# Low parts of weight pieces in the mixers: two GpSimd instructions of 512 columns in place of four of 256

## The chip, the cores and the metric

One core of a Trainium2 chip runs the kernel. Its engines are TensorE (PE; its weight loads are shown apart as PEld), VectorE (DVE), ScalarE (ACT), GpSimd (POOL) and SyncE (SP), which issues the loads. The metric is the device time of one execution in microseconds; the median of the runs shown stands for the kernel.

## The reference

The reference is a chain of two small transformer networks on one sequence of 256 tokens with a width of 1024, two layers each, all in float32:

```python
for l in range(2):                       # first network
    x = x + 0.5 * rmsnorm(swiglu(rmsnorm(x), w_gate, w_up, w_down))     # hidden width 2816
    x = x + rmsnorm(token_mixing(rmsnorm(x), w_in, ..., w_out))         # three kinds of attention
    x = x + 0.5 * rmsnorm(swiglu(rmsnorm(x), ...))
for l in range(2):                       # second network
    z = rmsnorm(x) @ w_in
    merged = sum(gate_i * (branch_i(z) @ w_branch[i]) for i in range(3))
    x = x + merged @ w_out
    x = x + square(relu(rmsnorm(x) @ w_up)) @ w_down                    # hidden width 4096
```

The token mixing of the first network has chunk band attention, differential attention and stick-breaking attention side by side. The three branches of the second network are a sparse attention (compressed, selected and window keys), a gated linear attention and an attention over 256 memory tokens. Nearly all of the work is in the products with the weights.

## The kernel before

All weights come as one stream of 616 pieces of 128 partitions x 1024 float32 columns, in the order in which they are used. SP loads a piece into one of 7 slots of `raw` (line 478). ScalarE rounds it to the format that TensorE multiplies fast and writes the result, the high part, into one of 5 slots of `hi` (line 1509). GpSimd subtracts the high part from the piece and writes what is left, the low part, into a slot of `lo` (lines 615, 624 and 634). Activations are split in the same way, and a product is made of three matmuls, high with high, high with low and low with high (`product`, lines 660 to 663); a piece takes 12 matmuls of 512 columns as a rule. TensorE waits for a piece by the semaphore `lo`; after its last matmul on it, it raises `used`, for which the slots of `raw` and `hi` wait.

Each engine runs a program of its own, written out in order; the semaphores tie them together. In a feed-forward stage the pieces follow one another with little else between them. In a mixer (a function `in_mixer` says which pieces these are, line 586) the steps of the attention are placed behind chosen pieces: TensorE makes scores, transposes and sums between the pieces, and VectorE and ScalarE do softmax and the like meanwhile. Where TensorE reaches such a step before its input is made, it waits, and the pieces behind it wait too.

Which part of a low part GpSimd makes in one instruction depends on the place: a whole piece of 1024 columns outside the mixers, halves for a few pieces at the beginning of stages (`by_halves`), and quarters of 256 columns in the mixers. In the first network's mixers (`c < L * PIECES1`) GpSimd also waits for its own quarter, by the semaphore `quarter`, before it issues the next one; in the second network's mixers quarters follow each other freely. At the start of each mixer piece it waits for the end of the piece before (line 630).

The steps of the second network's mixer that come up later: line 2562 subtracts the reference points of the decay of the gated linear attention (four instructions for each half of the levels), lines 2571 and 2572 multiply queries and keys by the decay, lines 2258 and 2262 (`normalise`) scale softmax rows by the inverse of their sums, line 2251 (`minima`) takes scores out of PSUM, line 935 is TensorE's transpose of the finished rows (`turn_blocks`), and line 2270 VectorE's copy of what it turned. Lines 2614 to 2623 are the activation of the compressed keys' hidden layer, which TensorE multiplies in line 1276. In the first network's mixer, line 2373 squares the output of the differential attention. Line 2849 belongs to the rotary angles, which are made in the last strips of a feed-forward stage.

Of the kernel before, what the change touches and what calls it, by code (L numbers as in the profile page):

```python
# [220 lines left out]
def f32(a):  # L221
    return a.bitcast(F32)
# [356 lines left out]
def half_width(c):  # L579

    at = (c - L * PIECES1) % PIECES2 if c >= L * PIECES1 else 0
    z3 = 4 * STRIPS2.index("z3")
    return WIDTH_Z3 if z3 <= at < z3 + 4 else PIECE // 2


def in_mixer(c):

    block, at = divmod(c, PIECES1) if c < L * PIECES1 else divmod(c - L * PIECES1, PIECES2)
    if c < L * PIECES1:
        return FFN_PIECES + 6 <= at < PIECES1 - FFN_PIECES - 4  # L590
    return 12 <= at < PIECES2 - 8 * MLP_STRIPS - KD - 4


def by_halves(c):

    if c < L * PIECES1:
        return c % PIECES1 in (FFN_PIECES + 3, PIECES1 - FFN_PIECES + 3) or c > PIECES1 and c % PIECES1 == 3
    at = (c - L * PIECES1) % PIECES2
    return at in (3, PIECES2 - 8 * MLP_STRIPS - 1, PIECES2 - 8 * MLP_STRIPS + 3)
# [7 lines left out]
def pool_program(M, V, sem):  # L607

    pool = M.nc.gpsimd
    for c in range(FIRST_HALVES):  # L610
        for i in range(2):
            w = slice(512 * i, 512 * i + 512)
            raw = M.raw[:, c, w] if c else V.first_weights[i]
            pool.wait_ge(sem["hi" if i else "half_hi"], c + 1)
            pool.tensor_tensor(M.lo[:, c, w], raw, f32(M.hi[:, c, w]), ALU.subtract).then_inc(
                sem["lo"] if i else sem["half_lo"], 1)
    quarters = 0
    for c in range(FIRST_HALVES, PIECES):
        slot, slot_hi = c % RING, c % RING_HI
        pool.wait_ge(sem["hi"], c + 1)  # L620
        if by_halves(c):
            for i in range(2):
                w = slice(512 * i, 512 * i + 512)
                pool.tensor_tensor(M.lo[:, slot, w], M.raw[:, slot, w], f32(M.hi[:, slot_hi, w]),
                                   ALU.subtract).then_inc(sem["lo"] if i else sem["half_lo"], 1)
            continue
        parts = 4 if in_mixer(c) else 1
        if parts == 4:

            pool.wait_ge(sem["lo"], c)  # L630
        for i in range(parts):
            whole = 2 * half_width(c)
            w = slice(i * whole // parts, (i + 1) * whole // parts)
            t = pool.tensor_tensor(M.lo[:, slot, w], M.raw[:, slot, w], f32(M.hi[:, slot_hi, w]), ALU.subtract)  # L634
            if i == parts - 1:
                t.then_inc(sem["lo"], 1)
            elif c < L * PIECES1:

                t.then_inc(sem["quarter"], 1)
                quarters += 1  # L640
                pool.wait_ge(sem["quarter"], quarters)
# [2275 lines left out]
def build(nc, T):  # L2917
    with ExitStack() as stack:
        M = memory(nc, T, stack)
        V = Views(M)  # L2920
        sem = {name: stack.enter_context(nc.semaphore("s_" + name)) for name in SEMAPHORES}
        landed = [stack.enter_context(nc.semaphore(f"s_landed{i}")) for i in range(RING)]
        sp_program(M, V, sem, landed)
        pool_program(M, V, sem)
        pe_program(M, V, sem)
        act_program(M, V, sem, landed)
        dve_program(M, V, sem)
# [151 lines left out]
```

## Time and profile before

| | us |
|---|---|
| median of 3 runs | 1880.04 |
| the runs | 1879.98 to 1880.36 |
| the profiled execution | 1880.13 |
| its span, first to last instruction | 1878.70 |

| engine | busy us | share of the span | instructions |
|---|---|---|---|
| PE matmuls | 1872.5 | 100% | 9604 |
| PE weight loads | 1549.8 | 82% | 9604 |
| VectorE | 1033.4 | 55% | 2654 |
| ScalarE | 1035.0 | 55% | 1765 |
| GpSimd | 1555.6 | 83% | 1102 |

The profile shows one execution. Times within it count from the start of the span. The shares are means over stages of different kinds; matmuls overlap, so a busy PE is not a measure of how fast it goes. The mean granted clock of TensorE is 1.000 in this execution. The mixers of the first network lie at about 201 to 282 us and 682 to 762 us, those of the second at about 994 to 1204 us and 1447 to 1658 us.

### The profile page before, as it was taken

The numbers are of one execution on the slowest core, as the hardware profiler recorded it, in microseconds if no ns is written. First come the engines' busy times: TensorE is split into PE (matmuls) and PEld (weight loads), VectorE is DVE, ScalarE is ACT, GpSimd is POOL, SyncE is SP. The second block draws the span as 40 slices with busy tenths as digits, with TensorE's granted clock in tenths as the row PEclk, the third lists the DMA queues.
The fourth block names the chain that finished last, engine by engine and source line by source line (L and its number), as shares of the span: only waits on it lengthen the run. The fifth ranks groups of instructions, "written<-read, shape, count | busy, mean of one in ns | idle before, by whom it ended". The sixth has DMA issues, their size and how long they took to land.

```text
span 1878.7 us, 27088 instructions
## 1 busy us (share of the span) xinstructions
PE 1872.5 (100%) x9604; PEld 1549.8 (82%) x9604; DVE 1033.4 (55%) x2654; ACT 1035.0 (55%) x1765; POOL 1555.6 (83%) x1102
## 2 busy tenths in 40 slices
PE   9999999999999999999999999999999999999999
PEld 8888887888888889788888877888888877788887
DVE  5338565434676756554344677446444477645542
ACT  7445666444744576654466454665456554566543
POOL 8988886988798878698879787779887968778986
DMA  7665444565565553367556343456657533345553
GB/s 285 243 231 182 166 135 157 192 198 192 204 236 196 190 169 135 132 220 261 196 187 255 124 146 117 154 184 220 235 191 260 169 126 133 124 165 194 192 197 138
DMA packets 98419, 348.94 MB, mean 186 GB/s; under 512 B 13260, under 2 KB 13932, under 8 KB 97772
## 3 DMA queue, kind: packets, MB, share of 16 engines
q1 hardware_dynamic: 97708, 346.06, 54.0%
q8 instruction: 77, 1.26, 0.3%
q10 hardware_dynamic: 576, 1.14, 0.2%
q14 instruction: 58, 0.48, 0.1%
HBM read 346.11 MB, written 1.05 MB: 185 GB/s over the span
## 4 chain that ended last, share of the span: by engine, by line
PE 99%; DVE 1%; ACT 0%; issue 0%; ACTq 0%
PE psum L661 28%; PE psum L663 28%; PE psum L662 28%; PE psum L689 1%; PE psum L691 1%; PE psum L692 1%; PE psum L945 1%; PE psum L759 1%; PE psum L935 1%; PE psum L958 1%; PE psum L1204 1%; PE psum L925 0%; PE psum L1361 0%; PE psum L1155 0%; PE psum L832 0%; PE psum L828 0%
## 5 line engine op out<-in xcount | busy, mean ns | idle before, releaser
L634 POOL TENSOR_TENSOR lo<-raw,hi 128x256 fp32r<-128x256 f32 (+2 forms) x1070 | 1520.4, 1443 | 298.3 <-ACT hi L1509 270.4
L1509 ACT ACTIVATE hi<-raw 128x1024 fp32r<-128x1024 f32 (+1 forms) x613 | 639.1, 1052 | 495.7 <-PE psum L663 461.6
L661 PE MATMUL psum<-hi,h_hi 128*128 128x512 f32 (+1 forms) x1504 | 592.6, 394 | 0.0
L663 PE MATMUL psum<-hi,h_lo 128*128 128x512 f32 (+1 forms) x1504 | 583.6, 388 | 0.0
L662 PE MATMUL psum<-lo,h_hi 128*128 128x512 f32 (+1 forms) x1504 | 583.0, 388 | 0.0
L2211 DVE STREAM_TRANSPOSE psum<-big 32x128 f32<-32x128 f32 (+1 forms) x960 | 344.0, 358 | 14.2
L661 PEld LDWEIGHTS psum<-hi,h_hi 128*128 128x128 f32 x1504 | 282.5, 188 | 59.0 <-issue 2.1
L663 PEld LDWEIGHTS psum<-hi,h_lo 128*128 128x128 f32 x1504 | 282.3, 188 | 58.9
L661 PE MATMUL psum<-hi,y_hi 128*128 128x512 f32 x832 | 328.1, 394 | 0.0
L662 PEld LDWEIGHTS psum<-lo,h_hi 128*128 128x128 f32 x1504 | 282.7, 188 | 54.8
L663 PE MATMUL psum<-hi,y_lo 128*128 128x512 f32 x832 | 324.3, 390 | 0.0
L662 PE MATMUL psum<-lo,y_hi 128*128 128x512 f32 x832 | 323.9, 389 | 0.0
L2220 DVE TENSOR_TENSOR y_lo<-psum,y_hi 128x512 fp32r<-128x512 f32 x76 | 51.0, 689 | 327.8 <-ACT y_hi L1635 327.4
L661 PEld LDWEIGHTS psum<-hi,y_hi 128*128 128x128 f32 x832 | 156.2, 188 | 34.5 <-issue 2.5
L663 PEld LDWEIGHTS psum<-hi,y_lo 128*128 128x128 f32 x832 | 156.2, 188 | 33.1
L662 PEld LDWEIGHTS psum<-lo,y_hi 128*128 128x128 f32 x832 | 156.3, 188 | 31.1
L2199 DVE SCALAR_TENSOR_TENSOR big<-psum,small,big 128x256 f32<-128x256 f32 (+1 forms) x120 | 61.0, 550 | 87.9 <-ACT big L1625 87.8
L1675 ACT ACTIVATE soft<-soft,small 128x128 f32<-128x128 f32 (+1 forms) x104 | 47.2, 455 | 78.3 <-DVE small L2251 57.5
L1625 ACT ACTIVATE big<-psum,small 128x256 f32<-128x256 f32 (+1 forms) x120 | 57.3, 529 | 53.9 <-PE psum L663 53.8
L2270 DVE COPY soft<-psum 128x384 f32<-128x384 f32 (+1 forms) x52 | 29.8, 573 | 49.3 <-PE psum L935 49.3
L689 PE MATMUL psum<-h_hi,hi 128*128 128x256 f32 x192 | 56.1, 292 | 0.0
L691 PE MATMUL psum<-h_lo,hi 128*128 128x256 f32 x192 | 54.3, 283 | 0.0
(355 smaller groups left out, 1599.4 us busy)
## 6 DMA issues: line engine op xcount, KB each, us to landing
raw<-in_stream SPq DMA_DIRECT2D x607, 512.0 KB, 3.4
big<-in_w SPq DMA_DIRECT2D x14, 512.0 KB, 7.1
big<-in_post SPq DMA_DIRECT2D x6, 512.0 KB, 4.7
special<-in_b_merge SPq DMA_DIRECT2D x2, 1536.0 KB, 7.4
raw<-in_stream SPq DMA_DIRECT2D x8, 296.0 KB, 5.6
memkv<-in_mem_turned SPq DMA_DIRECT2D x2, 1024.0 KB, 6.9
big<-in_band SPq DMA_DIRECT2D x2, 768.0 KB, 4.9
raw<-in_first SPq DMA_DIRECT2D x2, 512.0 KB, 4.1
```

Of the source, the lines that this page charges most:

```text
L634: t = pool.tensor_tensor(M.lo[:, slot, w], M.raw[:, slot, w], f32(M.hi[:, slot_hi, w]), ALU.subtract)
L661: pe.matmul(out, lhs_hi, rhs_hi, start=start, stop=False)
L662: pe.matmul(out, lhs_hi, rhs_lo, start=False, stop=False)
L663: return pe.matmul(out, lhs_lo, rhs_hi, start=False, stop=stop)
L689: pe.matmul(out, hi[:, slot_hi, w], h_hi[:, k, :], start=k == 0 and block % 2 == 0, stop=False, skip_group_check=True)
L691: pe.matmul(out, hi[:, slot_hi, w], h_lo[:, k, :], start=False, stop=False, skip_group_check=True)
L1509: act.activation(M.hi[:, slot_hi, used], M.raw[:, slot, used], ACT.Copy).then_inc(sem["hi"], 1)
L1625: t = act.activation(act_s[:, m, :], psum[:, bank + m, 0:width], ACT.Silu if gated else ACT.Relu, scale=V.scale[:, m:m + 1])
L1675: t = act.activation(prob[:, w], prob[:, w], ACT.Exp, scale=-1.0, bias=mn[:, i:i + 1], accum_out=total[:, i:i + 1])
L2199: t = dve.scalar_tensor_tensor(prod_s[:, m, :], psum[:, bank + m, col:col + width], V.scale[:, m:m + 1], act_s[:, m, :], ALU.mult, ALU.mult)
L2211: t = dve.transpose(dst[32 * b:32 * b + 32, :, :, 32 * a:32 * a + 32], src[32 * a:32 * a + 32, :, :, 32 * b:32 * b + 32])
L2220: dve.tensor_tensor(flat(y_lo[:, kt:kt + 2, :]), psum[:, bank + g, :], f32(flat(y_hi[:, kt:kt + 2, :])), ALU.subtract).then_inc(sem["ylo"], 1)
```

## The change

In the mixers, a low part is made in two instructions of half the piece each in place of four of a quarter each. The waits in the loop stay as they are written: in the first network one wait for the own first half is left of three for own quarters.

```diff
-        parts = 4 if in_mixer(c) else 1
-        if parts == 4:
+        parts = 2 if in_mixer(c) else 1
+        if parts == 2:
 
             pool.wait_ge(sem["lo"], c)
         for i in range(parts):
```

## Rows read from the trace of the kernel before

**Rows 1.** The page, part 1: busy time, share of the span, instructions of each engine.

```profile
PE 1872.5 (100%) x9604; PEld 1549.8 (82%) x9604; DVE 1033.4 (55%) x2654; ACT 1035.0 (55%) x1765; POOL 1555.6 (83%) x1102
```

**Rows 2.** Timeline (start us, us, engine, line, operation) of PE, then PEld, at 301.

```profile
300.68 0.39 PE L662 MATMUL psum<-lo,y_hi 128*128 128x512 f32 x1
...
302.26 0.39 PE L663 MATMUL psum<-hi,y_lo 128*128 128x512 f32 x1
...
301.13 0.19 PEld L662 LDWEIGHTS psum<-lo,y_hi 128*128 128x128 f32 x1
```

**Rows 3.** Waits over the span: engine, line <- releaser: us in all, times, longest.

```profile
POOL lo L634 <- ACT hi L1509: 270.4, 229, 7.6
...
PEld psum L1276 <- DVE extra L2623: 1.5, 2, 0.8
...
PEld psum L689 <- POOL lo L634: 0.7, 2, 0.3
```

**Rows 4.** GpSimd's groups by shape: xcount | busy us, mean ns | idle before them.

```profile
L634 POOL TENSOR_TENSOR lo<-raw,hi 128x256 fp32r<-128x256 f32 x624 | 464.1, 766 | 114.5 <-ACT hi L1509 87.2 <-POOL lo L634 0.4
L624 POOL TENSOR_TENSOR lo<-raw,hi 128x512 fp32r<-128x512 f32 x22 | 28.0, 1294 | 6.3 <-ACT hi L1509 6.3
```

**Rows 5.** Timeline of GpSimd at 1092.55 us, one quarter.

```profile
1092.55 0.74 POOL L634 TENSOR_TENSOR lo<-raw,hi 128x256 fp32r<-128x256 f32 x1 [3.88 <-ACT hi L1509]
```

**Rows 6.** Timeline of GpSimd and VectorE in a feed-forward stage, at 562.6 us.

```profile
562.61 2.40 POOL L634 TENSOR_TENSOR lo<-raw,hi 128x1024 fp32r<-128x1024 f32 x1 [0.32 <-ACT hi L1509]
...
562.63 2.44 DVE L2849 SCALAR_TENSOR_TENSOR extra<-extra 128x48 f32<-128x48 f32 x1
```

**Rows 7.** Summaries of two lines: xcount, shortest/median/longest ns, first to last start.

```profile
L2849 DVE SCALAR_TENSOR_TENSOR extra<-extra x3: 207/1917/2444, 560.4 to 562.6; 128x48 f32<-128x48 f32 x3
...
L2373 DVE TENSOR_TENSOR special<-special x2: 846/860/874, 236.0 to 716.8; 128x512 f32<-128x512 f32 x2
```

**Rows 8.** Timeline of the second network's first mixer, 1054.3 to 1057.3 us.

```profile
1054.35 2.84 POOL L634 TENSOR_TENSOR lo<-raw,hi 128x256 fp32r<-128x256 f32 x4 [1.02 <-ACT hi L1509]
...
1054.49 0.67 DVE L2621 TENSOR_SCALAR extra<-extra 128x128 f32<-128x128 f32 x1
...
1055.20 0.95 DVE L2622 RECIPROCAL extra<-extra 128x128 f32<-128x128 f32 x1
...
1056.19 0.42 DVE L2623 TENSOR_TENSOR extra<-extra 128x128 f32<-128x128 f32 x1
...
1056.66 0.41 PE L1276 MATMUL psum<-special,extra 128*32 128x64 f32 x4 [0.51 <-DVE extra L2623]
```

**Rows 9.** VectorE's groups, 1083 to 1107 us: xcount | busy, mean ns | idle before.

```profile
L2572 DVE TENSOR_TENSOR big<-big,kT 128x1024 f32<-128x1024 f32 x2 | 3.5, 1756 | 0.0
```

**Rows 10.** Summary of line 2562, 1083 to 1088 us, columns as in rows 7.

```profile
L2562 DVE TENSOR_TENSOR big<-extra x4: 942/950/960, 1083.8 to 1086.4; 128x256 f32<-128x256 f32 x4
```

**Rows 11.** Timelines of GpSimd, VectorE and PE, 1082 to 1110 us.

```profile
1082.13 6.54 POOL L634 TENSOR_TENSOR lo<-raw,hi 128x256 fp32r<-128x256 f32 x8 [5.18 <-ACT hi L1509]
...
1093.29 0.85 DVE L2262 TENSOR_SCALAR soft<-soft,small,extra 128x256 f32<-128x256 f32 x1
...
1094.77 0.33 PE L935 MATMUL psum<-consts,soft 128*128 128x128 f32 x1
...
1105.31 0.87 DVE L2262 TENSOR_SCALAR soft<-soft,small,extra 128x256 f32<-128x256 f32 x1
...
1108.68 0.27 PE L935 MATMUL psum<-consts,soft 128*128 128x128 f32 x1
...
1109.21 0.56 DVE L2270 COPY soft<-psum 128x384 f32<-128x384 f32 x1 [2.48 <-PE psum L935]
```

**Rows 12.** Timelines of GpSimd, VectorE and PE, 1145 to 1149 us.

```profile
1145.67 2.91 POOL L634 TENSOR_TENSOR lo<-raw,hi 128x256 fp32r<-128x256 f32 x4 [7.59 <-ACT hi L1509]
...
1147.16 0.83 DVE L2262 TENSOR_SCALAR soft<-soft,small,extra 128x256 f32<-128x256 f32 x1
...
1148.29 0.27 PE L935 MATMUL psum<-consts,soft 128*128 128x128 f32 x1
```

## The prediction

> **What bounds the kernel now.** I read the shares of the engines first [rows 1]. TensorE (PE) is busy for 100% of the span, but a busy share says little where matmuls overlap, so the second view is a timeline of PE in a stretch without waits [rows 2]: from 300.68 to 302.26 us seven matmuls of 512 columns start, one every 0.226 us, each shown 0.39 us long. I take that pitch as PE's floor; the clock stands at its upper level all along, since the mean granted clock of the profiled run is 1.0.
>
> The Trainium skill, page "Trainium Kernel Development and Optimization", section "Performance Expectations", calls matmul busy time a bad metric and LDWEIGHTS busy share a good one; by that rule the 82% of [rows 1] would leave up to 18% to win. The trace speaks against it here: in [rows 2] a weight load takes 0.19 us of a pitch of 0.226, which is 83% with nothing waiting, so 82% over the span is the floor too.
>
> Third come the waits [rows 3]. GpSimd (POOL) waits 270.4 us for ScalarE's high parts, so it is ahead of its supply. PE waits for GpSimd's low parts 0.7 us in all. The longest wait of PE's weight loads for another engine is that of line 1276 for VectorE (DVE): 1.5 us in two times. So PE sets the end, and a change to GpSimd moves the time only through instants at which PE waits for VectorE or GpSimd. There is next to nothing to win, and something to lose where a hand-over to PE is tight.
>
> **What is removed and added.** The trace has 624 quarter instructions of 766 ns and, from pieces that are done by halves already, 22 of 512 columns of 1294 ns [rows 4]. 156 pieces are meant: 624 x 0.766 = 478 us go and 312 x 1.294 = 404 us come, so GpSimd has 74 us less to do. I count this at nothing: it lies beside PE, GpSimd waits for ScalarE longer than that now, and PE's waits for it are 0.7 us, which is all that could be won. If that cover were gone, a piece would still come sooner than before (2 x 1.29 against 4 x 0.74 [rows 5] or more), so it can't cost. In the first network's mixers one wait of GpSimd for its own quarters stays per piece where three were; nothing but GpSimd's next instruction is queued behind it. No DMA is moved: GpSimd issues none, and SP's loads wait for PE's use of a piece, not for GpSimd.
>
> **What gets longer: the time in which GpSimd shuts VectorE out.** Rows of the feed-forward stretch show it alone [rows 6, 7]: line 2849, 128x48, takes 207 ns undisturbed and 2444 ns when it starts 0.02 us after a GpSimd instruction of 2.40 us; it ends at 565.07, 0.06 us after that one. So a VectorE instruction of that kind (two operands in SBUF, or a plain SBUF-to-SBUF one) waits until the GpSimd instruction under way is over. An undisturbed quarter is 0.74 us, a half 1.29 [rows 4]; a wait that begins near the start of one grows by 0.55 us.
>
> The Trainium skill, page "SBUF — State Buffer", section "SBUF: two separate sides", says the same as a rule, which speaks against this change: the pair of ports shared by GpSimd and VectorE is "an exclusive lock, not a bandwidth split", held for the whole instruction. With shared bandwidth the number of columns per instruction would not matter and the sum below would be 0.
>
> In the first network's mixers only line 2373 waits, twice in the run, 846 and 874 ns long [rows 7]; what follows it is not needed by PE soon. I count 0, and 0.1 us at most. The second network's mixers (994 to 1204 us, and the same again from 1447) have three places; I read them in the first.
>
> Place one, around 1054 [rows 8]. Line 2621 starts 0.14 us into a quarter and lasts 0.67, to 1055.16; line 2622 takes 0.95; line 2623 starts at 1056.19, waits for the third quarter, which ends at about 1056.46 (a piece takes 2.84, so quarters start 0.70 apart), and ends at 1056.61; PE's line 1276, idle for 0.51 us, starts 0.05 us later. With halves from the same start (ScalarE's high part sets it) the first ends at 1055.64, so 2621 ends 0.55 later; 2623 then starts at 1056.74, and the second half ends at 1056.89, so 2623 ends at about 1057.04. PE idles already, so all of it counts: **0.43 us**. Bounds: 0 (the second wait vanishes and GpSimd starts late) and 0.55.
>
> Place two, 1083 to 1107. VectorE is without a pause: the 11 groups of its instructions there show 0.0 or 0.1 us idle before them, as the row in [rows 9] does, so each delay is handed on. GpSimd starts two pieces at 1082.13 and works until 1088.67 [rows 11]; line 2562's four instructions run from 1083.8 to 1087.35 with one quarter between each two [rows 10]. Halves end at about 1083.4, 1084.8, 1086.4 and 1087.8 (0.17 more for each VectorE instruction let in: line 2562's starts lie (1086.4 - 1083.8) / 3 = 0.87 apart, against 0.70 of a quarter); 2562 gets in after the second, third and fourth, the last one follows freely, and they end at 1088.4: 1.1 late. Then GpSimd starts at 1092.55 [rows 5]; its second half ends at 1095.1, and line 2262's pair, which ended at 1094.14, ends at 1095.5: 1.36 late [rows 11]. PE's transposes of line 935 need it and start at 1094.77, 0.63 after it: PE loses 0.73. Between that and line 2262's end at 1106.18, five more VectorE instructions wait for GpSimd now (lines 2571, 2572, 2262, 2572, 2262): 5 x 0.55 = 2.75, together 4.1 late, 1110.3. PE needs that one at 1108.68, now 1109.41: another 0.88. Sum **1.6 us**. Bounds: 0.5 (only the first loss, with two of the later five waits grown) and 3.5 (every wait grows by 0.55, those of 2562 too). I take the walk, since its instants come from rows; the ends of pieces, where GpSimd waits for its own semaphore (line 630) and VectorE can slip in, cut it below the upper end. Little is late after that: VectorE now sits idle for 2.48 us before its next copy [rows 11], which waits for the same transposes.
>
> Place three, around 1147 [rows 12]: GpSimd starts at 1145.67, so the second half ends at 1148.2; line 2262's second instruction, which ended at 1147.99, ends at 1148.4, and PE's line 935 at 1148.29 is 0.1 late. Bounds 0 and 0.6. **0.1 us**.
>
> Sum per mixer 0.43 + 1.6 + 0.1 = 2.15, and for two mixers 4.3 us. The profiled execution took 1880.13 us (span 1878.70 and 1.43 around it), 0.09 over the median of the runs, 1880.04. **1880.1 + 4.3 = 1884.4 us.** By the bounds 1880.1 + 2 x 0.5 = 1881.1 to 1880.1 + 2 x 4.65 = 1889.4. No loss is counted for PE's pitch: nothing in the trace ties it to the length of GpSimd's instructions.
>
> **Rivals.** (1) The delays of place two are absorbed: only place one counts, 0.43 x 2, and the time is 1881.0. For it: the first need has 0.63 us and the last 2.5 us of room [rows 11]; a shift of the start by some tenths, or one more pause of GpSimd, is enough. Against it: VectorE has no idle time there. (2) Place two costs its upper end, the others as forecast: 2 x (0.43 + 3.5 + 0.1) = 8.1, 1888.2. For it: 2562's four and the later waits each meet a fresh instruction in the trace of before; against it: with halves there are fewer of them to meet.
> (3) The other side, not slower: GpSimd, done with a piece in 2 x 1.29 us and not in 2.84, sits idle when VectorE comes, and waits vanish. Place one decides: VectorE waits there until 1055.09 and 1056.46, 0.60 and 0.27 us, more than PE's idle 0.51, which would go, 1.0 us in two mixers; the time is 1879.1. It decides from the point at which GpSimd would be through before 1054.49, but there it had been idle for 1.02 us and starts with ScalarE's high part at 1054.35 [rows 8], whatever it did before. (4) The change doesn't do what it says, and GpSimd shuts VectorE out no longer than before: 1880.1. Against it: instructions of 512 and 1024 columns of this form are in the trace, and the longest one held VectorE for all its 2.40 us [rows 6].
>
> **Chances.** The forecast has 0.52, rival 1 0.20, rival 2 0.16, rivals 3 and 4 together 0.12. A measurement of this kernel can tell about 0.2% from no change, 3.8 us, so slower begins at 1883.8. Seven tenths of the forecast's own case (1882 to 1887) and all of rival 2 lie above: 0.36 + 0.16 = 0.52 slower. Faster needs more than PE waits for in all, 0.03. The rest, 0.45, is the same. The range of 8 in 10 runs from rival 1, a little under, to the upper bound: 1880.8 to 1889.4.
>
> **What would show it.** Right: GpSimd has 312 more instructions of 512 columns near 1.3 us, and no fewer idle times; line 2621 takes about 1.2 us and PE's idle before line 1276 grows from 0.51 to about 0.9; line 2562's four in the busy place take about 1.4 us each and line 935's weight loads show waits for line 2262 of 0.7 to 0.9 us in two places; PE's pitch stays 0.226. Wrong: line 2562 or 2262 as short as before, PE's waits for VectorE unchanged, or lost time in the first network's mixers, where I count none. A new wait of PE for low parts would speak against the first part of the sum.

## The result and the profile after

| | before | after |
|---|---|---|
| median, us | 1880.03 | 1886.90 |
| the runs, us | 1879.98 to 1880.36 (6) | 1886.64 to 1887.12 (6) |
| the profiled execution, us | 1880.13 | 1886.64 |

The ratio is 1.0037, with an interval of 1.0027 to 1.0046: slower by 6.87 us, 0.37%, where 4.3 us were forecast and the range went from 1880.8 to 1889.4 us.

GpSimd did what the change says. Its groups by shape in the profile after (count | busy us, mean ns | idle before them), beside [rows 4]:

```profile
L634 POOL TENSOR_TENSOR lo<-raw,hi 128x512 fp32r<-128x512 f32 x312 | 413.2, 1340 | 169.1 <-ACT hi L1509 152.1 <-POOL lo L634 0.4
```

312 halves stand for the 624 quarters, GpSimd works 464.1 - 413.2 = 51 us less on them, and idles more before them (169.1 us, where it was 114.5). PE got nothing from that. Its waits for another engine in the profile after (us in all, times, longest):

```profile
PE psum L935 <- DVE soft L2262: 4.7, 6, 1.5
PE psum L1276 <- DVE extra L2623: 1.9, 2, 0.9
...
PE psum L661 <- POOL lo L634: 0.2, 1, 0.2
```

Line 935 waited for line 2262 nowhere before; line 1276's wait rose from 1.0 us (PE's own idle time) to 1.9. The one wait for a low part lies at 28 us, ahead of all mixers; nothing speaks of low parts that come late in them. So the time went where VectorE hands something to PE. How much at which place is read from the instants of the same PE instructions in the two timelines; first before, in the first of the two mixers, just ahead of it and behind it, and behind the second:

```profile
971.72 0.55 PE L759 MATMUL psum<-consts,x 128*128 128x128 f32 x3
...
1222.10 0.27 PE L759 MATMUL psum<-consts,big 128*128 128x128 f32 x1
...
1676.50 0.60 PE L759 MATMUL psum<-consts,big 128*128 128x128 f32 x4
```

and after, with that wait at 28 us and the three places between (those of before are in [rows 8, 11, 12]):

```profile
28.12 0.47 PE L661 MATMUL psum<-hi,h_hi 128*128 128x512 f32 x1 [0.17 <-POOL lo L634]
...
971.32 0.66 PE L759 MATMUL psum<-consts,x 128*128 128x128 f32 x4
...
1056.66 0.41 PE L1276 MATMUL psum<-special,extra 128*32 128x64 f32 x4 [0.94 <-DVE extra L2623]
...
1096.38 0.33 PE L935 MATMUL psum<-consts,soft 128*128 128x128 f32 x1 [1.47 <-DVE soft L2262]
...
1111.09 0.33 PE L935 MATMUL psum<-consts,soft 128*128 128x128 f32 x1 [0.64 <-DVE soft L2262]
...
1151.16 0.33 PE L935 MATMUL psum<-consts,soft 128*128 128x128 f32 x1 [0.24 <-DVE soft L2262]
...
1225.04 0.27 PE L759 MATMUL psum<-consts,big 128*128 128x128 f32 x1
...
1683.01 0.38 PE L759 MATMUL psum<-consts,big 128*128 128x128 f32 x2
```

| PE instruction | before | after | shift, us | lost since the row above | forecast |
|---|---|---|---|---|---|
| line 759, ahead of the mixer | 971.72 | 971.32 | -0.40 | | |
| line 1276, place one | 1056.66 | 1056.66 | 0.00 | 0.40 | 0.43 |
| line 935, place two, first need | 1094.77 | 1096.38 | 1.61 | 1.61 | 0.73 |
| line 935, place two, last need | 1108.68 | 1111.09 | 2.41 | 0.80 | 0.88 |
| line 935, place three | 1148.29 | 1151.16 | 2.87 | 0.46 | 0.1 |
| line 759, behind the mixer | 1222.10 | 1225.04 | 2.94 | 0.07 | 0 |
| line 759, behind the second mixer | 1676.50 | 1683.01 | 6.51 | 3.57 | 2.15 |

The last shift, 6.51, is the whole difference of the two profiled executions, 1886.64 - 1880.13. The first, -0.40, is not the change's doing: the execution after is 0.51 us ahead at 28 us already (28.12 for 28.63), in the first feed-forward stage, where nothing was changed. Without it the losses add up to 6.91 us, close to the 6.87 between the medians. The places are those of the forecast; two of the four terms are too small.

### The profile page after: what moved, and what is told of

It reads as the page before. It is cut to its first block, busy times and chain, and to the rows that moved or that the text cites. A ratio compares the mean times of both kernels' runs of the same rounds, so it can differ in the third digit from the quotient of the medians.

```text
span 1885.2 us, 26776 instructions
## 1 busy us (share of the span) xinstructions
PE 1872.9 (99%) x9604; PEld 1548.2 (82%) x9604; DVE 1051.7 (56%) x2654; ACT 1034.9 (55%) x1765; POOL 1504.9 (80%) x790
## 4 chain that ended last, share of the span: by engine, by line
PE 93%; DVE 4%; issue 1%; ACT 1%; DMA 1%; POOL 0%; SPq 0%; DVEq 0%; ACTq 0%
PE psum L661 27%; PE psum L663 27%; PE psum L662 27%; PE psum L689 1%; PE psum L691 1%; PE psum L692 1%; PE psum L759 1%; PE psum L945 1%; PE psum L935 1%; PE psum L1204 1%; PE psum L958 1%; DVE soft L2262 0%; DVE big L2572 0%; DVE big L2562 0%; PE psum L925 0%
## 5 line engine op out<-in xcount | busy, mean ns | idle before, releaser
L634 POOL TENSOR_TENSOR lo<-raw,hi 128x1024 fp32r<-128x1024 f32 (+2 forms) x758 | 1469.7, 1958 | 356.0 <-ACT hi L1509 338.5
L692 PE MATMUL psum<-h_hi,lo 128*128 128x256 f32 x192 | 54.3, 283 | 0.0
```

The costliest lines, as they stand in the source:

```text
L692: t = pe.matmul(out, lo[:, slot, w], h_hi[:, k, :], start=False, stop=k == KD - 1, skip_group_check=True)
```

## Why place two cost more: timelines of 1082 to 1096 us

GpSimd, VectorE and ScalarE in the profile after:

```profile
1082.12 5.40 POOL L634 TENSOR_TENSOR lo<-raw,hi 128x512 fp32r<-128x512 f32 x4 [5.48 <-ACT hi L1509]
1093.67 18.66 POOL L634 TENSOR_TENSOR lo<-raw,hi 128x512 fp32r<-128x512 f32 x11 [6.15 <-ACT hi L1509]
...
1082.60 0.87 DVE L2682 TENSOR_TENSOR small<-small,extra 128x16 f32<-128x16 f32 x1
1083.50 1.45 DVE L2683 TENSOR_TENSOR extra<-extra,small 128x256 f32<-128x256 f32 x1
1084.87 3.60 DVE L2562 TENSOR_TENSOR big<-extra 128x256 f32<-128x256 f32 x4
...
1093.93 2.40 DVE L2262 TENSOR_SCALAR soft<-soft,small,extra 128x128 f32<-128x128 f32 x2
...
1088.72 0.40 ACT L1675 ACTIVATE soft<-soft,small 128x128 f32<-128x128 f32 x1 [5.73 <-DVE small L2251]
...
1092.55 1.99 ACT L1509 ACTIVATE hi<-raw 128x1024 fp32r<-128x1024 f32 x2
```

and the same in the profile before, where [rows 11] have the rest:

```profile
1082.61 0.31 DVE L2682 TENSOR_TENSOR small<-small,extra 128x16 f32<-128x16 f32 x1
...
1082.96 0.91 DVE L2683 TENSOR_TENSOR extra<-extra,small 128x256 f32<-128x256 f32 x1
1083.80 3.57 DVE L2562 TENSOR_TENSOR big<-extra 128x256 f32<-128x256 f32 x4
...
1087.61 0.40 ACT L1675 ACTIVATE soft<-soft,small 128x128 f32<-128x128 f32 x1 [4.61 <-DVE small L2251]
...
1091.43 1.99 ACT L1509 ACTIVATE hi<-raw 128x1024 fp32r<-128x1024 f32 x2
```

Lines 2682 and 2683, which the forecast did not have on its list, each meet a half and grow by 0.56 and 0.54 us. Line 2562's four begin 1.07 late and take as long as before in all. ScalarE waits for what VectorE makes next, the scores of line 2251, and goes on 1.11 us late (line 1675, 1087.61 to 1088.72); it reaches its high parts 1.12 us late (line 1509, 1091.43 to 1092.55), and so GpSimd starts at 1093.67, not at 1092.55. The forecast left that start where it was, so that VectorE, late by itself, would have met the halves late and been done soon after them. In fact both came late together, and line 2262's pair met two whole halves where it had met two quarters: it took 2.40 us, in place of 1.32 (from 1092.82 to 1094.14). The pair ended at 1096.33, 1.1 + 1.1 = 2.2 us late; 0.63 of it was spare, and PE lost 1.6.

At place three the pair was in the same position to GpSimd as before (1.23 us behind its start), but the first of the two did not get in between the halves. GpSimd's two halves, and the summary of line 2262's pair (count, shortest/median/longest ns), in the profile after:

```profile
1148.14 2.56 POOL L634 TENSOR_TENSOR lo<-raw,hi 128x512 fp32r<-128x512 f32 x2 [8.47 <-ACT hi L1509]
```

```profile
L2262 DVE TENSOR_SCALAR soft<-soft,small,extra x2: 402/908/1414, 1149.4 to 1150.7; 128x128 f32<-128x128 f32 x1, 128x256 f32<-128x256 f32 x1
```

The first of the pair took 1414 ns, the second 402. The second half ends 2.56 us behind the start, as forecast (2.5); what was wrong is that not one but both of the pair ended behind it.

## Experiments

Each is the kernel before or after with an edit of the rule for the number of instructions. The code is cut to that rule: `at`, the number of a piece within its layer of the second network, is computed in a line of its own above it, and the test below it (`parts == 4` or `parts == 2`) becomes `in_mixer(c)`, so that GpSimd waits for the end of the piece before at the start of every mixer piece, as ever. Edits that add lines move the later ones by one (by three where a wait is added), so line 1276 appears as 1277 or 1279.

The theory of places says: a half costs only where VectorE meets it and PE needs the result soon. The rival says that halves cost PE a little everywhere. The two are told apart by where the halves are.

**Quarters at the three places, halves elsewhere.**

```diff
-        parts = 2 if in_mixer(c) else 1
+        parts = (4 if at in (31, 37, 38, 39, 40, 41, 42, 53) else 2) if in_mixer(c) else 1
```

> The changed kernel with quarters kept for 8 of the 56 mixer pieces of each layer of the second network: number 31 of the layer (place one), 37 to 42 (place two) and 53 (place three). Theory of places (a half costs only where VectorE's two-operand steps meet it and TensorE is near): 1880.6 us, 1880.0 to 1881.2; line 1276 and line 935 wait as in the kernel before. Theory of a spread cost (each of the 156 pieces made by halves costs the same, 6.87 / 156 = 0.044 us): 1886.9 - 16 x 0.044 = 1886.2.

Measured: 1880.78 us, ratio 1.0003 (0.9995 to 1.0012). PE's waits:

```profile
PE psum L936 <- DVE big L2582: 1.2, 2, 0.6
...
PE psum L1277 <- DVE extra L2624: 1.1, 2, 0.5
PE psum L1205 <- issue: 0.5, 2, 0.3
```

Line 1277's wait is as before, and line 936 waits for line 2582 as before (1.2 us in two times) and for line 2263 no more. 140 of 156 pieces by halves cost 0.7 us by the medians, which the interval can't tell from nothing; line 1205's idle 0.5 us, which the kernel before does not show, is most of it.

**Halves at those places alone.**

```diff
-        parts = 4 if in_mixer(c) else 1
+        parts = (2 if at in (31, 37, 38, 39, 40, 41, 42, 53) else 4) if in_mixer(c) else 1
```

> The kernel before with halves for the same 8 pieces of each layer of the second network alone. Theory of places: 1886.5 us, 1885.5 to 1887.2. Theory of a spread cost: 1880.0 + 16 x 0.044 = 1880.7.

Measured: 1885.75 us, ratio 1.0030 (1.0019 to 1.0042). 16 pieces of 156 bring 5.71 of the 6.87 us, a little less than I expected. PE's waits:

```profile
PE psum L936 <- DVE soft L2263: 3.6, 5, 1.5
PE psum L1277 <- DVE extra L2624: 1.9, 2, 0.9
```

Five waits for line 2263 in place of six: one of the two last needs of place two is missing, so its size depends on the pieces around these as well.

**Halves in the first network only.**

```diff
-        parts = 4 if in_mixer(c) else 1
+        parts = (2 if c < L * PIECES1 else 4) if in_mixer(c) else 1
```

> Halves in the first network's mixers only (44 pieces), quarters in the second's. Theory of places: 1880.0 us, at most 0.3 from the kernel before. Spread cost: 1880.0 + 44 x 0.044 = 1881.9.

Measured: 1879.79 us, ratio 0.9999 (0.9990 to 1.0008). Line 2373, the only one that waits there, grew by 0.2 us and no more:

```profile
L2373 DVE TENSOR_TENSOR special<-special x2: 1058/1058/1058, 236.2 to 717.1; 128x512 f32<-128x512 f32 x2
```

PE does not need it soon, as forecast. Of GpSimd's three waits per piece for its own quarters two went here, and that brought nothing either.

**The cause doubled: whole pieces.**

```diff
-        parts = 4 if in_mixer(c) else 1
+        parts = 1 if in_mixer(c) else 1
```

> The suspected cause doubled: one instruction of 1024 columns (2.40 us) per mixer piece. If the loss goes by the length of the instruction that VectorE meets: 1880.0 + 6.87 x (2.40 - 0.74) / (1.29 - 0.74) = 1900.8 us; more where the last spare time is used up, so 1896 to 1910. If GpSimd, which has then still less to do, is mostly idle when VectorE comes: no more than for halves, 1887 or less.

Measured: 1899.32 us, ratio 1.0103 (1.0089 to 1.0116), near the 1900.8 of the proportion, although GpSimd does less work still. PE's longest waits:

```profile
PE psum L1204 <- DVE small L2251: 4.4, 2, 2.2
PE psum L1276 <- DVE extra L2623: 4.1, 2, 2.0
PE psum L935 <- DVE soft L2262: 3.1, 2, 1.6
PE psum L945 <- DVE soft L2270: 2.7, 2, 1.3
```

and line 2621 with GpSimd beside it, in the timeline:

```profile
1055.05 2.38 POOL L634 TENSOR_TENSOR lo<-raw,hi 128x1024 fp32r<-128x1024 f32 x1 [1.76 <-ACT hi L1509]
...
1055.19 2.32 DVE L2621 TENSOR_SCALAR extra<-extra 128x128 f32<-128x128 f32 x1
```

Place one grows with the length of the instruction that VectorE meets, and lines 1204 and 945, which had time to spare before, have become late too. The agreement in size is partly luck, though. Line 935 waits for line 2262 in two instants and not in six, so not every place has grown. And some 3 of the 19.3 us are lost to TensorE's clock. Its granted clock was 0.53 of full from 1171.0 to 1173.4 us, just behind its idle 2.18 us at line 1204, and 0.50 from 1523.5 to 1526.0, just behind its idle 2.05 us at line 1276 of the second layer. These are stretches at the lower of its two levels, and the matmuls there take 1.6 and 1.5 us longer than the same ones of the kernel before. The same two idles in the other layer were not followed by such a stretch.

**The disputed step: is the delay of 1083 handed on to GpSimd's start at 1092?** Once with quarters at the two pieces from 1082 on and halves elsewhere, once the other way round.

```diff
-        parts = 2 if in_mixer(c) else 1
+        parts = (4 if at in (37, 38) else 2) if in_mixer(c) else 1
```

> The changed kernel with quarters kept for the two pieces that GpSimd makes from 1082.1 us on (numbers 37 and 38 of each layer of the second network). If the delay of VectorE there is handed on to ScalarE and from it to GpSimd's next start (1093.67 in place of 1092.55), GpSimd starts at 1092.55 again, line 2262's pair, which ended 2.66 us after that start, ends at 1095.2, TensorE loses 0.5 us and not 1.6 at its first need, and line 1317 does not wait: 2 x (1.1 + 0.16) less, 1884.4 us. If the halves from 1092 on make that loss by themselves: 1886.9 - 2 x 0.16 = 1886.6.

Measured: 1884.97 us, ratio 1.0027 (1.0016 to 1.0038). Timelines of GpSimd, VectorE and PE:

```profile
1092.46 4.97 POOL L635 TENSOR_TENSOR lo<-raw,hi 128x512 fp32r<-128x512 f32 x3 [3.88 <-ACT hi L1510]
...
1092.72 2.42 DVE L2263 TENSOR_SCALAR soft<-soft,small,extra 128x128 f32<-128x128 f32 x2
...
1095.20 0.33 PE L936 MATMUL psum<-consts,soft 128*128 128x128 f32 x1 [0.46 <-DVE soft L2263]
```

The start is back at 1092.46, the pair takes as long as with halves everywhere (2.42 us), but it ends 1.2 us earlier and PE idles 0.46 us for it, not 1.47. Of the 2.5 us that I expected to come back 1.9 did. The need itself went as expected, at some 0.5 us; but line 1317 had cost PE under 0.1 us in each layer of the changed kernel, not 0.16, and line 1205 (1204 in the changed kernel), late there in the second layer alone, now takes about 0.2 us in the first as well.

```diff
-        parts = 4 if in_mixer(c) else 1
+        parts = (2 if at in (37, 38) else 4) if in_mixer(c) else 1
```

> The kernel before with halves for those two pieces alone, numbers 37 and 38. If the delay of 1.1 us is handed on through ScalarE to GpSimd's next start: line 2262's pair is 1.1 us late, 0.63 of it is spare, TensorE loses 0.5 there and 0.16 at line 1317, 2 x 0.66 in all: 1881.3 us. If the halves from 1092 on make the loss by themselves: 1880.0 + 2 x 0.16 = 1880.3.

Measured: 1881.39 us, ratio 1.0008 (0.9999 to 1.0017). The interval includes 1, but all runs (1881.05 to 1881.84) lie above those of the kernel before beside them (1879.38 to 1880.68). The same timelines, with ScalarE's:

```profile
1081.88 5.41 POOL L635 TENSOR_TENSOR lo<-raw,hi 128x512 fp32r<-128x512 f32 x4 [5.18 <-ACT hi L1510]
1093.44 3.85 POOL L635 TENSOR_TENSOR lo<-raw,hi 128x256 fp32r<-128x256 f32 x4 [6.14 <-ACT hi L1510]
...
1093.71 1.31 DVE L2263 TENSOR_SCALAR soft<-soft,small,extra 128x128 f32<-128x128 f32 x2
...
1092.31 1.99 ACT L1510 ACTIVATE hi<-raw 128x1024 fp32r<-128x1024 f32 x2
...
1095.07 0.44 PE L936 MATMUL psum<-consts,soft 128*128 128x128 f32 x2 [0.38 <-DVE soft L2263]
```

Four halves 11 us earlier push ScalarE's high parts from 1091.43 to 1092.31 and GpSimd's next start from 1092.55 to 1093.44, though the execution ran a little ahead (1081.88 against 1082.13), and the pair, which takes its old 1.31 us, is late by as much. So both halves of the explanation hold: the delay is handed on through ScalarE, and the halves from 1092 on add their own 1.1 us. The two together cost more than one by one, since the spare 0.63 us can be used only once.

**Place one without the meeting.** GpSimd waits with piece 31 until VectorE is through line 2623; PE needs that piece some 12 us later. First with quarters, then with halves:

```diff
+        at = (c - L * PIECES1) % PIECES2 if c >= L * PIECES1 else -1
         parts = 4 if in_mixer(c) else 1
-        if parts == 4:
+        if in_mixer(c):
+            if at == 31:
+                pool.wait_ge(sem["cdve"], 8 * ((c - L * PIECES1) // PIECES2) + 3)

             pool.wait_ge(sem["lo"], c)
```

> The kernel before, in which GpSimd begins piece 31 of each layer of the second network only when VectorE is through line 2623 (place one); TensorE uses that piece 12 us later. If it is GpSimd that holds VectorE there, TensorE's wait of line 1276 (0.68 us over its pitch, twice) goes: 1880.0 - 1.35 = 1878.7 us. If VectorE's steps are as long without GpSimd: 1880.0.

Measured: 1878.74 us (1878.57 to 1879.11, the kernel before 1879.38 to 1880.68 beside it), ratio 0.9994 (0.9985 to 1.0003). Timelines of GpSimd, VectorE and PE at place one:

```profile
1055.85 2.21 POOL L637 TENSOR_TENSOR lo<-raw,hi 128x256 fp32r<-128x256 f32 x3 [2.83 <-DVE extra L2626]
...
1054.18 0.22 DVE L2624 TENSOR_SCALAR extra<-extra 128x128 f32<-128x128 f32 x1
1054.43 0.95 DVE L2625 RECIPROCAL extra<-extra 128x128 f32<-128x128 f32 x1
1055.42 0.29 DVE L2626 TENSOR_TENSOR extra<-extra 128x128 f32<-128x128 f32 x1
...
1055.77 0.41 PE L1279 MATMUL psum<-special,extra 128*32 128x64 f32 x4
```

Line 2621 (here 2624) takes 0.22 us and not 0.67, PE has no idle time before line 1276 (here 1279), and 1.2 us are gained, about what was expected. This version is the fastest of all that ran, by a step that the interval alone would not settle; the row of PE without its wait does.

The same wait in the changed kernel (the edit is the same, with 2 for 4):

> The changed kernel with the same wait of GpSimd before piece 31. If the meeting and not the halves as such costs the time of place one, 0.68 + 0.43 us go in each layer: 1886.9 - 2.2 = 1884.7 us. If halves cost there in another way: 1886.9, or 0.9 less at most.

Measured: 1884.87 us, ratio 1.0026 (1.0016 to 1.0036): 2.0 us of the 6.9 less, and line 1276 (here 1279) is not among PE's waits any more. Halves that VectorE doesn't meet cost nothing there.

**The other direction: eighths in the second network.**

```diff
-        parts = 4 if in_mixer(c) else 1
+        parts = (8 if c >= L * PIECES1 else 4) if in_mixer(c) else 1
```

> The other direction: eighths of 128 columns in the second network's mixers, quarters in the first's. VectorE meets shorter instructions, so line 1276's wait shrinks, by 0.2 to 0.5 us in each layer. But by the steps from 512 to 256 columns (1.25 to 0.70 us) an eighth takes 0.70 - 0.28 = 0.42 and a piece 8 x 0.42 + 0.14 = 3.5 us, against 2.96 by quarters and 2.72 that TensorE takes for one; the low part that comes 0.16 us ahead of its use at 1011 is then some 5 x 0.54 - 0.16 = 2.5 us late, and the ones at 1106 and 1109 (0.8 and 0.7 ahead) about 1.4. Together about 3 us a layer slower: 1886 us, 1883 to 1890. If only the length that VectorE meets counted: 1879.4.

Measured: 1886.78 us, ratio 1.0037 (1.0023 to 1.0051), as slow as halves and for the opposite reason. PE's waits:

```profile
PE psum L661 <- POOL lo L634: 4.3, 10, 0.6
```

and place one in the timeline:

```profile
1057.02 0.38 DVE L2621 TENSOR_SCALAR extra<-extra 128x128 f32<-128x128 f32 x1
```

VectorE is let in sooner (line 2621 takes 0.38 us), and PE now waits for low parts ten times: GpSimd, slowed by twice as many instructions (an eighth takes 0.49 us on the mean, a quarter 0.74), has become late.

## Why the prediction was right and where it was off

**What bounds the kernel**: right. 51 us less of GpSimd's work (74 were forecast, with halves of 1.29 us; they took 1.34 on the mean) changed nothing for PE, and all of the loss lies at hand-overs to PE, mostly from VectorE. One reading of [rows 3] was wrong and changed nothing: line 1276's 1.5 us are not the longest wait of PE's weight loads for another engine. Line 759 waits 2.9 us for VectorE, in ten times, and line 802, at the start, 1.1 us in one; both are the same after the change.

**The mechanism**: shown. Line 2621, which starts 0.14 to 0.16 us behind the start of a GpSimd instruction at place one, or with none under way, takes

| GpSimd instruction met | none | 128 columns | 256 | 512 | 1024 |
|---|---|---|---|---|---|
| line 2621, us | 0.22 | 0.38 | 0.67 | 1.22 | 2.32 |

with the work of GpSimd falling from the second column to the last. It is the length of the one instruction met that counts, and rival 4 falls with that. The Trainium skill ("SBUF — State Buffer", section "SBUF: two separate sides") calls the ports that the two engines share an exclusive lock, held for the whole instruction; the row agrees with it.

**Place one**: 0.43 forecast and 0.43 measured as PE's idle time ahead of line 1276 (0.51 to 0.94; the table has 0.40, since PE gained 0.03 us between its first two rows). The second of its waits vanished (line 2623 took 0.29 us, its time without GpSimd); the first one grew by the whole 0.55.

**Place two, first need**: this is the step that failed, 0.73 against 1.61. The text counted 1.36 us of delay for the pair, with GpSimd starting at 1092.55 as before. That GpSimd starts when ScalarE's high part comes was read from the trace; that ScalarE itself follows VectorE was not followed up. The later start adds 0.8 to the 1.36 (2.2 in all), and since the spare time was used up by then, all of it counted. The steps before it were off in detail and right in sum: line 2562's four did not grow, lines 2682 and 2683 did, and VectorE was 1.1 us late as forecast. That sum came right by luck, and line 2562 as short as before was one of the signs named for being wrong.

**Place two, last need**: 0.88 against 0.80. Line 2262's last instruction ended at 1111.04 in place of 1106.18; 4.86 less the 2.19 of the first pair is 2.67, for which the forecast had 5 x 0.55 = 2.75.

**Place three**: 0.1 against 0.46, because the first of the pair was taken to get in between two halves.

**The first network and the rest**: 0 forecast; halves there change nothing that can be measured. One wait was not foreseen, that of line 1204 in the second layer's mixer. In PE's timeline after it starts 0.50 us behind the matmul before it; in the kernel before it started 0.31 behind it:

```profile
1623.00 0.39 PE L663 MATMUL psum<-hi,h_lo 128*128 128x512 f32 x1
1623.50 0.46 PE L1204 MATMUL psum<-memkv,big 64*128 64x128 f32 x3
```

These 0.2 us are about the difference of the two layers, 3.57 and 3.34.

**Rivals**: rival 1 (absorbed) is out, since 2262's delay showed in full behind its spare time. Rival 2 (8.1 us) named the size better than the forecast did, 6.9 lies between the two, but not for its reason: not every wait grew. Line 2562's four took no longer in all, and line 2571 fell from 1.74 to 1.21 us in its first case. Rival 3 was right in one thing, that some waits vanish, but place one, which was to decide, went the other way.

## What to carry to other kernels

On an engine that shuts another one out, the size of one instruction is a price that its own timeline doesn't show: look for the neighbour's short steps on the path to the bound engine, and cut the instructions there, or keep them away from that instant by a wait that costs nothing where the result is needed much later. Shorter is not always better, since each instruction has its own cost; here 512 columns in the mixers and 128 in those of the second network both lost 7 us to 256. And when a delay is walked through a trace, move the starts of the other engines with it: what triggers them may be late for the same reason.

## Unexpected in the hardware's behaviour

Not every VectorE instruction between SBUF tiles waits for GpSimd: line 2622, a reciprocal of 128x128, took 0.95 us in the changed kernel, from 1055.33 on, with a half under way beside it until 1056.44, and 0.95 in the kernel where GpSimd stood still. Line 2628 (32x64), 0.21 us in the kernels before and after, where it met no GpSimd instruction, does wait: with whole pieces it started 0.38 us into a GpSimd instruction of 2.39 and took

```profile
1059.64 2.09 DVE L2628 CUSTOM_DVE_ANT_0 extra<-extra 32x64 f32<-32x64 f32 x1
```

The text of the prediction had sorted the instructions by their operands; what sorts them exactly stays open.
